# An MoE step on one core: overflow rows gathered ahead of the fourth scatter, waits on VectorE at their readers, hidden rows turned inside the next gate products

## What is computed

```python
D_MODEL, N_GROUPS, EXP_PER_GROUP, EXP_HIDDEN, TOP_K_INNER = 1024, 4, 4, 256, 2   # 16 experts

def _hmoe(h, rg_w, rg_b, re_w, re_b, wg, wu, wd):
    gl = (xf @ rg_w + rg_b).astype(F32)
    gsel = jnp.argmax(gl, -1)                       # one group of four
    gprob = jnp.max(jax.nn.softmax(gl, -1), -1, keepdims=True)
    el_sel = el[jnp.arange(n), gsel]
    top_v, top_i = lax.top_k(el_sel, TOP_K_INNER)   # two experts in it
    top_w = jax.nn.softmax(top_v, -1) * gprob
    ...
    hid = jax.nn.silu(jnp.einsum('nd,edf->nef', xf, wg)) * jnp.einsum('nd,edf->nef', xf, wu)
    hid = hid * comb[:, :, None].astype(hid.dtype)
    return jnp.einsum('nef,efd->nd', hid, wd).reshape(bsz, t, d)

# in _trunk, for each layer
x = _layer_norm(ALPHA * x + gt1 * y, ...)
h = x * (1 + sc2) + sh2
y = _hmoe(h, ...)
x = _layer_norm(ALPHA * x + gt2 * y, ...)
```

## Time and profile before

| | us |
|---|---|
| median of 3 runs | 990.42 |
| the three runs | 981.88, 990.42, 1000.48 |
| the profiled execution | 986.8 |
| its span, which all positions below refer to | 985.1 |
| PE busy | 881.2 (89%) |
| DVE, ACT, POOL busy | 366.6, 234.2, 183.3 |
| experts of layer 0, from the first gate product to the first `rows_turned` | 404.96 to 534.01 |
| the same in layer 1 | 820.86 to 949.15 |

### The profile page before, as it was taken

How to read it: one execution, slowest core, us unless ns; L and a number is a source line. 1 busy time by engine, 2 the same in 40 slices (tenths; PEclk the granted TensorE clock), 3 DMA queues, 4 the chain that set the end, 5 groups by cost and what they waited for, 6 DMA issues and landing times.

```text
span 985.1 us, 19004 instructions
## 1 busy us (share of the span) xinstructions
PE 881.2 (89%) x8134; PEld 614.4 (62%) x8134; DVE 366.6 (37%) x869; ACT 234.2 (24%) x532; POOL 183.3 (19%) x237
## 2 busy tenths in 40 slices
PE   4799999979989898999788999899999988997994
PEld 0577667859977675755455567566577756553553
DVE  0623340626442647411212616823231364111226
ACT  0211224323312414111010414123332131110104
POOL 0100001203190215412221310000000244221213
PEclk9899999989999899899989999979999988998997
DMA  9947220341044865379999986512746744899931
GB/s 365 392 154 291 89 86 11 104 182 66 23 158 180 354 270 209 137 305 409 426 425 381 387 358 261 187 71 96 275 190 258 314 165 171 320 424 428 421 138 49
DMA packets 29878, 234.64 MB, mean 238 GB/s; under 512 B 6439, under 2 KB 6983, under 8 KB 14657
## 3 DMA queue, kind: packets, MB, share of 16 engines
q1 hardware_dynamic: 20736, 211.50, 53.6%
q0 software_dynamic: 8592, 19.52, 5.4%
q10 hardware_dynamic: 464, 2.39, 0.7%
HBM read 223.36 MB, written 18.94 MB: 246 GB/s over the span
## 4 chain that ended last, share of the span: by engine, by line
PE 72%; DMA 11%; DVE 9%; issue 3%; ACT 2%; POOL 1%; SPq 0%; POOLq 0%; DVEq 0%; ACTq 0%
PE ps L711 18%; PE ps L1059 9%; PE ps L847 6%; PE ps L1106 4%; PE ps L693 4%; PE ps L1253 3%; PE ps L854 3%; PE ps L732 3%; DVE arena L1878 3%; DMA arena<-in_w 2%; DMA arena<-hbuf,IDXJ 2%; DMA arena<-zbuf 2%; DMA zbuf<-arena,IDXS 2%; DMA ring<-in_w 2%; PE ps L801 2%
## 5 line engine op out<-in xcount | busy, mean ns | idle before, releaser
L711 PE MATMUL ps<-arena,ring 128*128 128x288 f32 x832 | 210.2, 414 | 6.3 <-DVE arena L1573 3.8
L711 PEld LDWEIGHTS ps<-arena,ring 128*128 128x128 f32 x832 | 159.7, 194 | 57.0 <-issue 10.7
L1059 PE MATMUL ps<-arena 128*64 128x256 f32 x960 | 115.7, 394 | 10.3 <-DVE arena L1783 7.0
L1059 PEld LDWEIGHTS ps<-arena 128*64 128x64 f32 x960 | 75.5, 142 | 49.2 <-issue 21.5
L693 PE MATMUL ps<-con,arena 128*128 128x128 f32 (+2 forms) x350 | 57.5, 299 | 19.1 <-DMA arena<-hbuf,IDXJ 12.0
L693 PEld LDWEIGHTS ps<-con,arena 128*128 128x128 f32 (+2 forms) x350 | 42.0, 147 | 42.7 <-issue 17.9
L847 PE MATMUL ps<-arena 64*64 64x64 f32 x1888 | 63.3, 221 | 4.5 <-issue 3.7
L847 PEld LDWEIGHTS ps<-arena 64*64 64x64 f32 x1888 | 60.2, 137 | 10.1 <-issue 8.3
L2151 ACT ACTIVATE arena<-ps 128x128 f32<-128x128 f32 x36 | 10.0, 277 | 186.9 <-PE ps L1059 158.7
L1106 PE MATMUL ps<-arena 128*64 128x512 f32 x176 | 51.1, 598 | 0.8 <-DVE arena L1783 0.8
L2015 ACT ACTIVATE arena<-ps 128x288 f32<-128x288 f32 x40 | 16.1, 407 | 126.1 <-PE ps L711 112.7
(11 more groups left out here) (323 smaller groups left out, 1311.8 us busy)
## 6 DMA issues: line engine op xcount, KB each, us to landing
arena<-in_experts SPq DMA_DIRECT2D x30, 2048.0 KB, 16.7
ring<-in_w SPq DMA_DIRECT2D x24, 2048.0 KB, 8.7
arena<-in_w SPq DMA_DIRECT2D x16, 2048.0 KB, 13.5
arena<-in_experts SPq DMA_DIRECT2D x26, 1024.0 KB, 15.6
ring<-in_experts SPq DMA_DIRECT2D x6, 2048.0 KB
ring<-in_experts SPq DMA_DIRECT2D x10, 1024.0 KB, 13.2
zbuf<-arena POOLq DMA_DIRECT2D x2, 2304.0 KB, 17.6
arena<-zbuf SPq DMA_DIRECT2D x8, 512.0 KB, 7.1
```

Of the source, the lines that this page charges most:

```text
L711: last = mm(ps[:, tile % 4, 0:T], wslot[j][:, k, o * P:(o + 1) * P], rhs_at(k), start=k == 0, stop=k == KT - 1)
L1059: last = mm(ps[64 * j:64 * j + 64, 2 + b, 0:256], x(k), ewgu[slot][:, k, j * 256:(j + 1) * 256], start=k == 0, stop=k == KT - 1)
```

## The change

Four things are done.

1. PE turns the hidden rows of expert e-1 half way through the gate product of expert e (after 4 of its 8 k-steps), not behind it. U(12), the first product after the overflow pass, has none inside. In the overflow pass the first set is turned inside the second gate product, and the second set between the two down products.
2. POOL gathers the rows of the first overflow pass (`job_rows(base)`) just ahead of `send(3)`, not after `send(4)`.
3. On PE the wait for DVE's weighting of pair 5 (`y_dve`) stands ahead of the overflow pass's down products, no longer ahead of the pass. The wait for the weighting of the overflow results (`o_ydve`) stands ahead of D(6), no longer ahead of U(12).
4. On DVE `table(3)` comes after `step_h(0)` and `step_u(1)`, no longer before them.

```diff
-                def gate_up(slot, b, x):
+                def gate_up(slot, b, x, between=None):
                     for k in range(KT):
+                        if between and k == KT // 2:
+                            between()
                         for j in range(2):
...
-                def step_u(e):
+                def step_u(e, between=None):
...
-                    gate_up(slot(e), e % 2, lambda k: xselT[e // 2 % 2][:, k * P + c:k * P + c + C])\
+                    gate_up(slot(e), e % 2, lambda k: xselT[e // 2 % 2][:, k * P + c:k * P + c + C], between)\
                         .then_inc(s["gu_mm"], 1)
...
+                            def turned(b):
+                                pe.wait_ge(s["o_hid"], n * 2 + b + 1)
+                                turn_hidden(b).then_inc(s["o_ht_mm"], 1)
+
...
                                 gate_up(JSLOT[b], b,
-                                        lambda k: xselT[1][:, b * 512 + k % 4 * P + k // 4 * C:][:, 0:C])\
+                                        lambda k: xselT[1][:, b * 512 + k % 4 * P + k // 4 * C:][:, 0:C],
+                                        (lambda: turned(0)) if b else None)\
                                     .then_inc(s["o_gu"], 1)
-                            for b in range(2):
-                                pe.wait_ge(s["o_hid"], n * 2 + b + 1)
-                                turn_hidden(b).then_inc(s["o_ht_mm"], 1)
+                            pe.wait_ge(s["y_dve"], 2 * ((NPAIR - 1) * layer + NSCAT) + AHEAD)
                             pe.wait_ge(s["o_ydve"], n * 2 + AHEAD)
                             for b in range(2):
+                                if b:
+                                    turned(1)
                                 pe.wait_ge(s["o_ht"], n * 2 + b + 1)
...
-                        pe.wait_ge(s["o_ydve"], (np_ + base) * 2 + AHEAD)
...
                         step_d(e // 2 - 1)
-                        pe.wait_ge(s["y_dve"], 2 * ((NPAIR - 1) * layer + NSCAT) + AHEAD)
                         pe.wait_ge(s["xt_act"], 2 * (p0 + NSCAT + 1))
                         further_jobs()
-                    step_u(e)
+                    step_u(e, (lambda: step_h(e - 1)) if e and e != LATE else None)
                     if e < 2:
                         tables(2 + e)
-                    if e and e != LATE:
-                        step_h(e - 1)
                     if e % 2 == 0:
                         if e + 2 < NE:
                             step_t(e // 2 + 1)
+                        if e // 2 - 1 == NSCAT:
+                            with pe.If(np_ > 0):
+                                pe.wait_ge(s["o_ydve"], (np_ + base) * 2 + AHEAD)
                         if e and e != LATE:
                             step_d(e // 2 - 1)
...
                 for e in range(NE):
-                    if e == 1:
-                        table(3)
...
-                    if e == 0:
-                        table(2)
+                    if e < 2:
+                        table(2 + e)
...
+                    if p == 3:
+                        job_rows(base)
                     send(p)
...
-                    if p == 4:
-                        job_rows(base)
```

## The result

The changed kernel takes 979.15 us (median of 20 runs, 975.18 to 988.44), the kernel before 987.76 (20 runs, 980.02 to 1000.48) in the same comparison. The ratio is 0.9934, 95% interval 0.9912 to 0.9956: 6.5 us faster (4.3 to 8.7). The ratio is taken over the executions within 1.5% of the fastest of the same kernel, so it is not quite the ratio of the two medians. The same program was timed again later, beside other kernels; that gave 0.9991 (0.9957 to 1.0024). The two intervals do not meet, and no run here shows why: how much of the total time the change saves, 6.5 us or 0.9, stays open. What the traces show is that most of what varies lies outside the changed part: the spans of the two profiled executions of the changed kernel differ by 7.9 us (978.4 and 986.3), of which 1.1 lie in the two stretches that the change touches.

What follows compares the result with a forecast made beforehand. It took the full weight stream, not PE's idle time, to bound each layer's experts. 986.8 - 5.15 (stream earlier) + 2.6 (low clock at U(15)) = 984.2 us, or 986 from the middle of four executions; range 974 to 996.

Steps and rivals of the forecast that it cites:

- The bound: Each layer's experts end when the full weight stream ends, a block of fixed bytes; what counts is when it becomes continuous.
- D(0) earlier: Start of each layer's stream: D(0) ends 3.4 us earlier in layer 0, 1.75 in layer 1; 5.15 off, on the path.
- The clock's part: U(2) of layer 0: its slow run goes with the pause ahead of it, another 1.65 us off, called not certain.
- The rest of the stream: Weight loads from D(0) to U(15): a block of fixed bytes, so an earlier start moves its end equally.
- Hidden rows turned inside: Gate products of the expert pairs: 0.53 us off a pair, 2.1 up to D(5), but 0 on the path.
- the turn inside a product: A transpose between the running matmuls of a gate product: taken as 0.2 us, between 0.13 and 0.33.
- The overflow pass: Earlier gather: waits of 4.52 and 1.24 us go, pass ends at 496.7 instead of 509.5; gain returns as weight waits.
- the 10 us or more: Sign of being right: waits for weights ahead of U(12) to U(15) of this total in each layer.
- The clock at U(15): Last gate product runs partly at low clock after its wait: cost 0.95 and 1.65, 2.6 us on, bounds 0 and 6.2.
- the forecast 3.7: Wait for weights ahead of U(15) in layer 0, from 520.9 to 524.6, in us.
- The sum: Whole kernel: 5.15 us off for the earlier stream, 2.6 on for the clock, giving 984.2; chance 0.68.

Runs made afterwards that it cites:

- fewer bytes: Only the first quarter of the down weights of experts 6 to 15 and overflow jobs loaded; changed kernel 0.9732, kernel before 0.9975.
- `table(3)` alone: Kernel before with part 4 of the change alone, table(3) moved later on DVE; ratio 0.9995.
- overflow part only: Kernel before with parts 2 and 3 alone: overflow rows gathered earlier, waits for y_dve and o_ydve moved; ratio 1.0030.
- turns only: Kernel before with hidden rows turned inside the next gate product, outside the overflow pass only; ratio 1.0036.
- The filled kernel: Changed kernel with 9 matmuls that nobody reads ahead of U(14), to keep PE busy while it waits; one execution, 992.47 us.
- gather late: Changed kernel with the overflow rows gathered at the old place, after the fifth scatter; ratio 0.9986.

## Why the prediction was right, point by point

**The bound** was named rightly, and it is shown, not only argued: with the gather early or late (8 us apart at U(12)) U(15) stays; with fewer bytes it moves by 9 to 10 us in the changed kernel and not at all in the kernel before. The last part adds what the prediction did not say: before the change PE's own pauses were as much a bound as the stream. That the measured 979.15 us lies in the range of 974 to 996 shows little, since the kernel before, at 987.76, lies in it as well.

**D(0) earlier.** Forecast 3.4 and 1.75 us, measured 3.8 and 2.2 (24.6 and 22.9 to 20.7). That these are so near is in part luck: 0.95 of each is the pause in U(1) of the one profiled execution of before, which the forecast didn't know. Without it, and at full clock, the gain is 1.2 us (22.0 to 20.7) where 1.75 was forecast. The turn in U(1) costs 0.4 and not 0.2, and the one in U(2) I had not counted at all. The mechanism is part 4 of the change: `table(3)` alone gave 22.4 at the low clock, which is 20.8 without the 1.6 us that this cost. The clock's part, which I had called uncertain, holds: U(2) ran at the low clock in 6 of the 10 layers whose kernels kept a wait ahead of it (before, table(3) only, overflow part only, turns only, fewer bytes before), and in none of the 18 layers of the kernels without that wait.

**The rest of the stream.** From the end of D(0) to U(15) I took the stream as fixed. It was 98.5 and 100.1 us before, 97.3 and 98.6 after. In the other kernels that have the full bytes in the old order it was between 96.9 and 99.5. So with the same bytes it varies by 3.2 us, 96.9 to 100.1, and is not the fixed block that I took it for, and 1.2 and 1.5 us of this case's gain lie in that. Of this I can place only 0.24, the shorter first pair. The overflow part alone had 96.9 in layer 0 and 99.5 in layer 1. What decides within that range stays open.

**Hidden rows turned inside.** Forecast 0.53 us off a pair, measured 0.24 (12.58 to 12.34). The mis-sized term is the turn inside a product: I took 0.2 us, between 0.13 and 0.33. U(3) now takes 3.86 us from its start to that of what follows, where it took 3.56; U(4), an even one, 3.96 where it took 3.61: 0.30 and 0.35. It costs as much as a lone transpose, the upper bound. Off the path, as forecast.

**The overflow pass.** Forecast: D(5) at 483.0, U(12) ready at 496.7; measured 484.9 and 499.2 in an execution whose U(0) was 0.95 us later, so 1.0 and 1.5 off. The two gathers landed at 67.2 and 69.6 us from U(0), 9 us ahead of the end of D(5), and ahead of the scatter of pair 3, at 465.92, POOL still had 1.01 us of waiting for DVE, so the gathers did not hold it up. The time went where it was said to go: the waits are 1.53, 4.38 and 1.28 us in layer 0, 7.2 in all, and 8.2 in layer 1, less than the 10 us or more that I had named as the sign. U(12) did not wait, because its weights had landed.

**The clock at U(15)** is the step that failed, by the 2.6 us that it had in the sum. It measured nothing: U(15) took 4.1 us with its turn in both layers, at full clock, and again in both layers of the second profile. I had summed the waits ahead of U(13) to U(15) with every product at full speed. In fact the wait of 4.38 us ahead of U(14) brought the clock down at U(14),'s 0.50 again, U(14) took 5.45 and 5.56 us, and the wait ahead of U(15) shrank to 1.3. The filled kernel restored a wait of 2.7 there, and the low clock came in one layer of two. So the slow U(14) took 1.4 of the forecast 3.7, and 1.0 was never there: the weights of experts 14 and 15 became ready 10.2 us apart (107.9 and 118.1), where I had 11.0. A sum over waits that are taken as independent was the first mistake; the size of the wait was the second. Luck has its part too: in layer 1 of the second profile U(14) was fast, the wait 2.59, and U(15) still ran at full clock.

The Trainium skill (TensorE: Matmul & The Clock Gate, HAM oscillation — how this bites in real kernels) says that such waits throttle the engine anew each time. Among the experts of the traces here it held for every wait of 3.7 us and more, for some of 2.0 to 2.8, and not for those of 1.3 ahead of U(15). What decided here is that a slow product behind one transfer eats the wait for the next.

**The sum.** Forecast -5.15 + 2.6 = -2.6. Measured in the two stretches -8.7 in the first profile and -7.5 in the second, of which D(0) gives 6.0 (1.9 of that the pause in U(1) of the kernel before), the rest of the stream the remainder, and the clock at U(15) nothing. The timed change is -6.5 in one comparison and -0.9 in the other, with the forecast between them. The forecast of 986 us was 7 too high for the 979.15 measured.

## What to carry to other kernels

If a stream of transfers is full up to the last product, ask what made it full, and look there: removing waits in the middle only moves them. Before moving one transfer out of the way, write down what each following product waits for; here the next bound was 1 us behind the first. And compare with more than one profile of the kernel before: here its only one held a pause of 0.95 us a layer that none of its close relatives has. Where the runs differ by more than the change, compare distances inside one stretch of the trace from a common start, and look at both layers.

## What the runs showed of the hardware

- A wait of 0.5 to 1.9 us ahead of U(2), at the same place in nearly the same programs, was followed by the low clock (0.50, the level of 1.2 GHz) in some layers and not in others: 6 of 10. It cost 1.6 to 2.8 us each time. Removing such a wait removed that spread as well, which was worth about as much as the wait.
- The last 2 MB load of layer 0, counted from U(0), was issued 12.0 us earlier than before (88.0 instead of 100.0) into a full queue and landed 5.0 us earlier (118.1 instead of 123.1): 30.1 us to landing instead of 23.0.
- The same program differs between its two layers and between executions by where the low clock falls: U(0), behind a wait of 0.78 us, took 3.67 us in most layers and 5.37 or 5.38 in layer 1 of three kernels (overflow part only, gather late, before with fewer bytes).
- A lone 128x128 float32 transpose in the middle of a gate product costs 0.30 to 0.35 us in a steady pair (0.41 in U(1) and U(2)), two and a half times its share in a row of nine (0.13).
